# A weight split on GpSimd in four instructions of 512 columns in place of two of 1,024, in a two-layer transformer forward pass

## The reference, cut to what matters

```
h = rms_norm(x, norm1_g);  proj = h @ w_in                       # q, k, v, bg, cg, xc
x = x + (g_attn * (attention(q, k, v) @ w_attn_proj) + g_conv * (short_conv(bg, cg, xc) @ w_conv_proj)) @ w_out
x = x + square(relu(rms_norm(x) @ w_up)) @ w_down
for layer in (0, 1):                                             # the second module
    u = rmsnorm(h, ...)
    y = window attention with a sink (layer 0)  or  hgrn2, a gated linear recurrence over 8 heads (layer 1),
        each joined with cross attention to a memory of 256 tokens, then @ w_out
    h = h + rmsnorm(y)
    h = h + rmsnorm(conv_ffn(rmsnorm(h)))                        # gelu(dwconv(gate)) * up, @ w_out
```

## Time and profile before

| | |
|---|---|
| median of 3 runs | 2595.08 us (2591.63 to 2595.32) |
| the profiled execution's own time | 2592.62 us |
| its span in the trace | 2590.8 us |
| busy: PE, DVE, POOL, ACT | 95%, 53%, 53%, 23% |
| mean granted TensorE clock | 0.973 of full speed |
| moved from and to HBM | 212.6 MB, 82 GB/s |

### The profile page before, as it was taken

One profiled execution on the slowest core, in us unless ns is written; L12 is line 12 of the kernel. 1 busy time (PEld: TensorE's weight loads), 2 busy tenths in 40 slices (PEclk: granted clock), 3 DMA queues, 4 the chain that ended last, 5 costly groups with the idle time before them and its releaser, 6 DMA issues.

```text
span 2590.8 us, 32130 instructions
## 1 busy us (share of the span) xinstructions
PE 2455.5 (95%) x12288; PEld 2007.2 (77%) x12288; DVE 1370.8 (53%) x2007; ACT 588.2 (23%) x1196; POOL 1370.3 (53%) x773
## 2 busy tenths in 40 slices
PE   8999999999999999899899999898999977999997
PEld 6877778887888877787678888676888866788885
DVE  3336754335113225776388550356888883885502
ACT  3233321003002100454121110134444432211100
POOL 6554446666666664343456666534444424576661
PEclk9999999999999999899999999998999988999998
DMA  4222222222222321121122222211111111222221
GB/s 155 89 94 90 76 87 98 95 94 96 95 93 97 122 90 65 58 79 53 65 81 91 98 98 98 73 57 58 58 57 66 58 49 57 81 97 94 96 97 57
DMA packets 59755, 214.58 MB, mean 83 GB/s; under 512 B 6624, under 2 KB 6752, under 8 KB 59488
## 3 DMA queue, kind: packets, MB, share of 16 engines
q1 hardware_dynamic: 56880, 206.68, 23.4%
q10 hardware_dynamic: 2736, 5.96, 0.7%
HBM read 210.51 MB, written 2.10 MB: 82 GB/s over the span
## 4 chain that ended last, share of the span: by engine, by line
PE 77%; DVE 18%; ACT 2%; issue 2%; DMA 0%; DVEq 0%; SPq 0%; ACTq 0%
PE acc L542 21%; PE acc L544 21%; PE acc L543 21%; PE ps_s L676 2%; PE ps_o L704 2%; PE ps_t L690 2%; PE acc L743 1%; PE acc L744 1%; PE acc L745 1%; DVE hg_level_q L1982 1%; DVE hg_level_k L1982 1%; DVE normed L1459 1%; DVE hg_in L1505 1%; DVE x_res L1470 1%; DVE hg_in L1989 1%
## 5 line engine op out<-in xcount | busy, mean ns | idle before, releaser
L500 POOL CAST w_hi<-w_raw 128x1024 fp32r<-128x1024 f32 x384 | 423.2, 1102 | 1142.2 <-DMA w_raw<-stream 1142.2
L503 POOL TENSOR_TENSOR w_lo<-w_raw,w_hi 128x1024 fp32r<-128x1024 f32 x384 | 947.2, 2467 | 30.7
L542 PE MATMUL acc<-h_hi,w_hi 128*128 128x512 f32 (+1 forms) x1872 | 746.1, 399 | 21.5 <-DVE h_lo L1433 16.9
L544 PE MATMUL acc<-h_hi,w_lo 128*128 128x512 f32 (+1 forms) x1872 | 722.6, 386 | 0.0
L543 PE MATMUL acc<-h_lo,w_hi 128*128 128x512 f32 (+1 forms) x1872 | 721.8, 386 | 0.0
L542 PEld LDWEIGHTS acc<-h_hi,w_hi 128*128 128x128 f32 x1872 | 356.6, 190 | 100.4 <-DVE h_lo L1433 24.3
L544 PEld LDWEIGHTS acc<-h_hi,w_lo 128*128 128x128 f32 x1872 | 355.8, 190 | 72.2
L543 PEld LDWEIGHTS acc<-h_lo,w_hi 128*128 128x128 f32 x1872 | 356.8, 191 | 69.5 <-issue 3.6
L1481 DVE COPY y_all<-acc 128x512 f32<-128x512 f32 x32 | 22.1, 692 | 238.7 <-PE acc L544 237.7
L542 PE MATMUL acc<-hid_hi,w_hi 128*128 128x512 f32 x352 | 138.7, 394 | 0.0
L544 PE MATMUL acc<-hid_hi,w_lo 128*128 128x512 f32 x352 | 138.0, 392 | 0.0
(11 more groups left out here) (314 smaller groups left out, 3652.9 us busy)
## 6 DMA issues: line engine op xcount, KB each, us to landing
w_raw<-stream SPq DMA_DIRECT2D x384, 512.0 KB, 3.2
toeplitz<-ext_in ACTq DMA_DIRECT2D x16, 256.0 KB, 3.7
out<-x_res SPq DMA_DIRECT2D x4, 512.0 KB, 2.6
x_res<-x_in SPq DMA_DIRECT2D x3, 512.0 KB, 6.8
mem<-mem_in ACTq DMA_DIRECT2D x1, 1024.0 KB, 6.4
consts<-consts_in SPq DMA_DIRECT2D x1, 784.0 KB, 9.7
x_res<-x_in SPq DMA_DIRECT2D x2, 256.0 KB, 5.1
rope<-rope_in ACTq DMA_DIRECT2D x1, 512.0 KB, 7.4
```

Of the source, the lines that this page charges most:

```text
L500: nc.gpsimd.tensor_copy(hi, raw).then_inc(hi_made, 1)
L503: nc.gpsimd.tensor_tensor(lo, raw, f32(hi), ALU.subtract).then_inc(split_made, 1)
L542: nc.tensor.matmul(ps, hi, x_hi[:, k, 0:cols], start=(k == 0), stop=False)
L544: mm = nc.tensor.matmul(ps, lo, x_hi[:, k, 0:cols], start=False, stop=(k == st.kt - 1))
```

## The change

The two instructions over 1,024 columns become four over 512: both halves of `w_hi` first, then both halves of `w_lo`. The wait ahead of each half of `w_lo` is for its half of `w_hi`. `split_made` is counted up by the last of the four, so TensorE waits for the whole slot as before. The first half of `w_lo` counts up a semaphore that nobody waits for.

```diff
+        low_half = sem("low_half")
...
-                nc.gpsimd.tensor_copy(hi, raw).then_inc(hi_made, 1)
-
-                pool.wait_ge(hi_made, slot + 1)
-                nc.gpsimd.tensor_tensor(lo, raw, f32(hi), ALU.subtract).then_inc(split_made, 1)
+                for half in (slice(0, D // 2), slice(D // 2, D)):
+                    nc.gpsimd.tensor_copy(hi[:, half], raw[:, half]).then_inc(hi_made, 1)
+                pool.wait_ge(hi_made, 2 * slot + 1)
+                nc.gpsimd.tensor_tensor(lo[:, 0:D // 2], raw[:, 0:D // 2], f32(hi[:, 0:D // 2]), ALU.subtract).then_inc(low_half, 1)
+                pool.wait_ge(hi_made, 2 * slot + 2)
+                nc.gpsimd.tensor_tensor(lo[:, D // 2:], raw[:, D // 2:], f32(hi[:, D // 2:]), ALU.subtract).then_inc(split_made, 1)
```

## The result

| | before | after |
|---|---|---|
| median | 2594.91 us (2591.63 to 2595.32, 4 runs) | 2562.59 us (2561.74 to 2564.34, 4 runs) |
| span of the profiled execution | 2590.8 us | 2561.3 us |
| no matmul under way (span less PE busy) | 135.3 us | 117.1 us |
| mean granted TensorE clock | 0.973 | 0.978 |

The ratio is 0.9879, with a 95% interval of 0.9863 to 0.9895: 32 us faster. The forecast was faster, 2583 us, with a range of 2568 to 2598.

What follows compares the result with a forecast made beforehand. TensorE, 95% busy, was taken as the bound, idling where GpSimd's split holds up VectorE. Savings of 8.4 + 1.3 + 1.9 + 0.7 = 12.3 us gave 2583 us in terms of the median, range 2568 to 2598.

Steps and rivals of the forecast that it cites:

- What bounds the kernel: Whole kernel: TensorE is busy 95%; GpSimd's split is waited for once, at the start, but its instructions hold up VectorE.
- GpSimd's own time: Split on GpSimd: halves take 0.57 and 1.24 us, busy time rises to 1,390 to 1,450 us, hidden by load waits.
- The waits in an unbroken run: VectorE without pauses: four waits behind GpSimd sum to 2.36 us per slot, 0.43 less than 2.79.
- The hgrn2 layer: Eight TensorE idle stretches there lose 11.2 us; a quarter off for ScalarE or TensorE's own sequence leaves 8.4 us.
- The window attention: Six places with waits ahead of an idle TensorE, 0.43 us each, 2.6 us; halved to 1.3 us.
- Norms and feed-forward inputs: Two slots each at two places, 0.6 us a slot, 2.4 us; taken as 1.9 us.
- The start: First slots: split_made up to 0.2 us later, a held h_lo gives TensorE 0.9 us; 0.7 us less in all.
- A boundary between two GpSimd instructions is enough: Where GpSimd hands VectorE its turn: any boundary does, with nothing waited for, so the new ones between halves will do.
- Slower by the fixed cost: Rival: from f = 0.305 us per GpSimd instruction, VectorE's waits on its chain cost more; 2600 to 2608 us, chance 0.16.
- No measurable change: Rival: waits fall, but something nearly as late sets TensorE's idle stretches; 2590 to 2596 us, chance 0.22 including no effect.
- no effect: Rival: GpSimd holds VectorE over both halves where nothing is waited for between them; 2595 us, within the 0.22.
- The case of more: Rival: VectorE's runs break more often, lone instructions wait half as long, doubling the gain; 2568 to 2575 us, chance 0.17.

Runs made afterwards that it cites:

- the fill of 0.95 us: A memset filling w_lo with zeros replaced the subtraction, against the kernel before: 2526.82 us, ratio 0.9744.
- the best kernels here: Alternating w_hi and w_lo pieces, each w_lo waiting, slot 0 whole, against the kernel before: quarters 2536.66 us; eighths in two stages, quarters elsewhere, 2534.86 us.
- Two kernels with 13.4 and 13.1 us of idle time: The kernel before with only w_hi in halves, 2581.00 us, and the changed kernel with both in halves, 2562.59 us; window stretch.

## Why the prediction was wrong, point by point

In short: the mechanism was right as far as VectorE's waits and TensorE's idle time, and the sum was too small in two places. It priced only idle time, at 12.3 us, where 18.2 went. And it had no term for the clock, where TensorE's busy time fell by 11.3 us with the matmuls unchanged.

- **What bounds the kernel: right.** Nobody waits for GpSimd but once, and VectorE waits for it. The changed kernel shows the once: its first matmul begins at 9.27 us, where it began at 9.05, the 0.2 us as forecast.
- **GpSimd's own time: the price of a half was low.** 0.57 and 1.24 us forecast, 0.60 and 1.26 measured; the fixed part is 0.17 us and not the memset's 0.10. Its busy time of 1514 us passed my 1,450 mainly for that: 768 x 0.169 = 130 us of fixed part, where I had 77. It waits 999 us for loads, where I had 1,050 to 1,120.
- **The waits in an unbroken run: right in form.** 2.36 us forecast, 2.55 measured, 2.79 before. The part of each GpSimd instruction that does not hold VectorE up, some 0.3 us, is there four times, as I had it. VectorE's busy time fell by 109 us in the whole, over my 30 to 80.
- **The hgrn2 layer: the step that failed most.** 8.4 us forecast for the eight idle stretches; its stretch of the run, with five of them, got 16.2 us shorter. In order of time the eight stretches lost 1.6, 2.7, 2.7, 1.4, 2.7, 0.6, 0.8 and 0.2 us, 12.6 in all, where I had 2.1, 2.0, 2.0, 1.4, 2.0, 0.4, 0 and 1.3, 11.2 in all. So the idle time was priced nearly right, and the quarter that I took off it had no ground. The 2.0 us per head was low: VectorE's busy time fell by 21.4 us in that stretch, and three idle stretches of 2.7 us went altogether. What was missing is the next step: 6.2 of the 16.2 us are no idle time at all; they are matmuls that had run at the lower clock. The other three of the eight lie behind that stretch, where 2.1 us less of idle time made the stage only 0.3 us shorter.
- **The window attention: mis-sized by six.** 1.3 us forecast, 7.4 measured in its stretch. Idle time gave 3.5 us, so halving the six places was wrong as well; the other 3.9 us are busy time, and the granted clock rose from 0.95 to 0.99. The prediction has no term for the clock anywhere in its sum, and names it only in the rival that is slower. Over the whole run idle time fell by 18.2 us and busy time by 11.3, the 29.5 us of the span. I had 12.3 for the first and nothing for the second.
- **Norms and feed-forward inputs: the size came out by luck.** 1.9 us forecast; the two feed-forward input stages (slots 196 to 239 and 318 to 361) are 0.8 and 0.9 us shorter. But the idle stretch that I had named, of 2.27 us, is 2.37 us now, and the idle time of the two stages together did not fall (5.1 and 3.5 us before, 4.4 and 4.2 after):

```profile
1300.70 0.50 PE L545 MATMUL acc<-h_hi,w_hi 128*128 128x512 f32 x1 [2.37 <-DVE h_lo L1436]
```

- **The start: 0.7 forecast, 2.6 measured.** I priced one of two idle stretches. The one of 1.67 us is gone altogether and another, of 1.14 us, is now 0.60.

```profile
9.27 0.79 PE L746 MATMUL acc<-w_hi,h_hi 128*128 128x512 f32 x1 [9.27 <-POOL w_lo L506]
19.88 0.50 PE L746 MATMUL acc<-w_hi,h_hi 128*128 128x512 f32 x1 [0.60 <-DVE h_lo L1594]
```

- **"A boundary between two GpSimd instructions is enough": true of this change, and false as a rule.** With halves it held. With 256 columns and no pause in between, 20 boundaries in a row did not do. Had the change been one to quarters, that step would have cost 12 us at the start.
- **The rivals.** Slower by the fixed cost fell (f is 0.17 us; at 0.305 it would have begun; the four waits sum to 2.16 + 2f rather than 2.18 + 2f, which makes that 0.315; and its range stops at the plain 13 us, where 13 us doubled would give 2621). No measurable change and no effect fell. The case of more had the right sign and too little: it too counted waits and no clock.
- **The Trainium skill's estimate of the fixed part** (GPSIMD Engine Reference, Elementwise — side-by-side cycle accounting; an estimated 193 ns from its 4497 ns) was nearer to the measured 169 ns than the memset row that I took; the time that it gave, some 2587 us, was further off, since the terms above were missing there too. The rule that only a GpSimd instruction that reads contends with VectorE's two SBUF inputs (SBUF — State Buffer, Who interferes with whom) agrees with the rows at the fill of 0.95 us: `hg_level_q` and `hg_level_k` took 0.43 and 0.42 us under it, and 1.14 us where they met `w_hi`.

## What to carry to other kernels

An engine that nobody waits for can still cost time, through another engine that stands while it reads: look for one form of instruction with two durations, and for what began just before the longer one. Cut such background work in pieces. With halves no more was needed; with quarters and eighths look for long waits of the other engine, and if there are any, let the pieces of the two kinds alternate, each waiting for the one before, as the best kernels here did. Do it first in the stages in which the other engine is what TensorE waits for; elsewhere it gave nothing. When a change takes away idle stretches of TensorE, price the slower matmuls behind them as well: here they were 11.3 of 29.5 us, some two fifths of the gain.

## What the runs showed of the hardware that was not expected

- **GpSimd in line can keep VectorE out.** Without a pause between its instructions, from 256 columns down, VectorE instructions stood for 10.84 and 13.89 us above their own time at the start, and with eighths for 2.0 to 3.0 us in six of the eight heads. With the same lengths in alternating order, and a pause of 0.08 us ahead of each `w_lo`, none stood for over 0.6 us, but for the one behind the whole slot 0. Which of the two does it, and why 20 boundaries at the start did not let VectorE in while in steady work two at most were passed with quarters, stays open.
- **A fill holds up one form and not another.** Under a memset of 0.95 to 1.04 us a `tensor_tensor` with two inputs in SBUF took its own 0.42 us, and a `tensor_scalar` took 1.18 us instead of 0.40.
- **The fixed part of a GpSimd instruction** that reads is 0.17 to 0.18 us at each length, by doubling and subtracting: `w_hi` took at least 0.28, 0.39, 0.60 and 1.04 us and `w_lo` 0.45, 0.71, 1.26 and 2.35 us for 128, 256, 512 and 1,024 columns.
- **Equal idle time, unequal clock.** Two kernels with 13.4 and 13.1 us of idle time in the same stretch ran it at 0.94 and 0.99 of full speed, and one is 6.2 us longer. What decides it was not tried.
